# Ten weight places for the first two rounds, and the embedding products in the last group of experts

## The chip, the cores and the metric

The kernel runs on one core of a Trainium2 chip. Each core has five engines with instruction streams of their own: TensorE (PE, matrix products, with its weight loads shown as PEld), VectorE (DVE), ScalarE (ACT), GpSimd (POOL) and SyncE (SP). SP issues nearly all transfers here; sixteen DMA engines carry them out, in the order in which SP's queue hands them over. Engines meet through semaphores. Data on chip lie in SBUF (128 partitions), and matrix products are written to eight PSUM banks of 128 x 512 fp32.

The metric is the time of one execution in microseconds (us) on the device. It is given as a median of timed runs; a separate, profiled execution gives the trace.

## What is computed

256 tokens of width 1024, all in fp32, one layer:

```python
h = rms_norm(x, norm_mix_g)
proj = h @ w_in
x = x + concat([s5_mixer(proj[:, :512]), rwkv7_mixer(h, ...)]) @ w_out
# 32 experts, the best 4 for each token
hf = rms_norm(x, norm_moe_g)
logits = hf @ router_w + router_b
top_v, top_i = top_k(logits, 4);  gates = softmax(top_v)
for e in experts:                       # for the tokens that chose e
    gt  = minimum(xb @ w_gate[e] + b_gate[e], 7.0)
    up  = clip(xb @ w_up[e] + b_up[e], -7.0, 7.0)
    act = (up + 1.0) * gt * sigmoid(1.702 * gt)
    yb  = act @ w_down[e] + b_down[e]
    x  += gates[e] * yb
# the embedding of the layer, p is 256 x 256
gate = sigmoid(rms_norm(x, norm_ple_g) @ ple_w_gate)
x = x + (p @ ple_w_proj) * gate
out = rms_norm(x, final_norm_g)
```

An expert's three matrices are 1024 x 1024 fp32, 4 MB each. All 32 experts are read: 384 MB. (MB and KB are the profile's binary ones where a transfer's size is meant: 2048 KB is 2,097,152 bytes.)

## The kernel before

**Stages.** First the two mixers (a long program of small products), the output projection, the turned residual stream `x2T`, and the router's logits. Then `route_tensor`, `route_vector` and `route_scalar` choose the best four experts for each token and count the tokens. Then the experts run one after another. Then comes a tail: the third norm, the gate product with `ple_w_gate`, the last norm and the output.

**One expert** is `expert` in `expert_tensor` on PE: 16 contraction steps of gate products, 16 of up products, a `scatter` of the expert before into the banks 0 to 3 (they hold the sum over all experts until the tail), turns, a `gather` of the next expert's tokens, and 16 steps of down products. Each product with weights is written in two column halves of 64 tokens by 512. The first four experts are written out, groups 1 to 6 run in a loop on the register `q`, and the last four are written out again (group 7).

**Weights** come in chunks of 2 MB, half of a matrix: two of `w_gate`, two of `w_up`, two of `w_down` for each expert, so 192 chunks in all, numbered in the order of their use from 0. `arena` is one SBUF tile cut into 47 units of 4 KB per partition. `RING` names eight places of four units (`slot(0)` to `slot(7)`). A ninth place, `extra`, is made of the units 24, 25, 26 and 29 and is used once, for chunk 8: three quarters are issued in L358, the last in L1490 once the four embedding products are done, for unit 29 is a part of their weights. From chunk 9 on, `expert_sync` waits on SP until an earlier chunk is used (`chunks_used`, counted by PE) and issues the next one into its place: chunk i for i from 9 to 16 waits until i - 8 chunks are used, later ones until i - 7 are used.

**Before the experts** SP's order is: chunks 0, 4 and 5; the embedding's `pT` and `wproj`; the input again; chunk 1 after the recurrence (L348); chunks 6 and 7 after `mix_rw_ready` (L352); chunks 2 and 3 after the output projection (L355); the three quarters of chunk 8 after the logits (L358). The places of a later one overlap with data that the mixers still need.

**The embedding products** `ple_proj(n)` compute p @ ple_w_proj in four pieces of 128 x 512, two contraction steps each (the trace counts four fp32 instructions for one). Piece 2 stands on PE ahead of the second half of the logits, pieces 3 and 0 at the head of `route_tensor`, piece 1 in `open_outputs` behind the first expert's up products. ScalarE's `copy_ple` (L1343) moves each from its bank to SBUF, and `open_outputs` waits for all four copies, since it reuses the banks 0 to 3 for the down bias. Right behind it the first expert also runs a `scatter` of zeros.

**Small tiles.** The routing tables, `gT`, `pg`, `xg` and `y` of the experts lie in the units 37, 38 and 40.

## Time and profile before

| | |
|---|---|
| median of 3 timed runs | 1180.39 us (1180.38 to 1183.22) |
| profiled execution, its own time | 1182.24 us |
| its span in the trace | 1180.4 us |
| PE busy | 1104.3 us (94% of the span) |
| DVE, ACT busy | 359.5 us, 198.6 us |
| moved by DMA | 430.58 MB (decimal), mean 365 GB/s |
| mean granted TensorE clock | 0.998 of full speed |

The span is the trace from its first to its last instruction; the profiled execution's own time holds 1.84 us more that lies around it. A stretch of the span is named by its start and end in us. A row of the timeline gives start, duration, engine, line and operation; "idle before" is how long the engine stood still ahead of it, and what released it. SPq is SP's DMA issue: the duration there is that of issuing, not of the transfer. A row xN merges N instructions, and its duration then reaches from the first's start to the last's end. A window's row gives each engine's busy time with instruction counts, the granted clock of PE (1.00 is full speed), the busy share of the sixteen DMA engines and what they moved.

### The profile page before, as it was taken

The numbers are of one execution on the slowest core, as the hardware profiler recorded it, in microseconds if no ns is written. First come the engines' busy times: TensorE is split into PE (matmuls) and PEld (weight loads), VectorE is DVE, ScalarE is ACT, GpSimd is POOL, SyncE is SP. The second block draws the span as 40 slices with busy tenths as digits, with TensorE's granted clock in tenths as the row PEclk, the third lists the DMA queues.
The fourth block names the chain that finished last, engine by engine and source line by source line (L and its number), as shares of the span: only waits on it lengthen the run. The fifth ranks groups of instructions, "written<-read, shape, count | busy, mean of one in ns | idle before, by whom it ended". The sixth has DMA issues, their size and how long they took to land.

```text
span 1180.4 us, 16582 instructions
## 1 busy us (share of the span) xinstructions
PE 1104.3 (94%) x7042; PEld 480.1 (41%) x7042; DVE 359.5 (30%) x745; ACT 198.6 (17%) x318; POOL 5.8 (0%) x11
## 2 busy tenths in 40 slices
PE   9999999999999999999999999999999999999987
PEld 8788974433333333333333333333333333333334
DVE  7987745312222222212111222222111111111123
ACT  6761322310110000000000000000000000000022
POOL 0100000000000000000000000000000000000000
PEclk9999999999999999999999999999999999999999
DMA  9402284899999999999999999999999999999970
GB/s 325 134 2 78 88 328 154 362 393 401 428 428 428 428 427 429 429 428 428 429 429 429 428 428 429 429 428 428 429 429 428 428 428 431 428 426 428 428 300 36
DMA packets 44844, 430.58 MB, mean 365 GB/s; under 512 B 4992, under 2 KB 15616, under 8 KB 20096
## 3 DMA queue, kind: packets, MB, share of 16 engines
q1 hardware_dynamic: 44608, 429.40, 87.2%
q8 instruction: 36, 0.59, 0.2%
q0 software_dynamic: 192, 0.52, 0.1%
q14 instruction: 8, 0.07, 0.0%
HBM read 428.86 MB, written 1.05 MB: 364 GB/s over the span
## 4 chain that ended last, share of the span: by engine, by line
PE 50%; DMA 44%; DVE 4%; ACT 1%; issue 1%; SPq 0%; DVEq 0%; ACTq 0%
PE bank L1321 34%; DMA arena<-in_exp_w_up 24%; DMA arena<-in_exp_w_gate 19%; PE bank L249 13%; PE bank L1383 1%; DVE arena L638 1%; PE bank L1632 1%; PE bank L1628 1%; DMA arena<-in_xT 0%; ACT arena L475 0%; PE bank L984 0%; DVE arena L882 0%; DVE arena L629 0%; DVE arena L632 0%; PE bank L266 0%
## 5 line engine op out<-in xcount | busy, mean ns | idle before, releaser
L1321 PE MATMUL bank<-arena 128*64 128x512 f32 (+3 forms) x3808 | 849.7, 588 | 59.1 <-DMA arena<-in_exp_w_up 52.0
L1321 PEld LDWEIGHTS bank<-arena 128*64 128x64 f32 (+3 forms) x3808 | 272.4, 140 | 591.1 <-issue 471.6
L249 PE MATMUL bank<-arena 64*64 64x64 f32 (+8 forms) x2104 | 170.7, 265 | 7.1 <-issue 3.6
L249 PEld LDWEIGHTS bank<-arena 64*64 64x64 f32 (+3 forms) x2104 | 137.0, 146 | 35.9 <-issue 18.5
L1517 ACT ACTIVATE cc<-arena 128x512 f32<-128x512 f32 x32 | 20.2, 630 | 459.7 <-DVE arena L1562 459.7
L1567 DVE TENSOR_SCALAR arena<-bank 128x512 f32<-128x512 f32 x32 | 22.1, 692 | 219.9 <-PE bank L1321 219.9
L1364 DVE TENSOR_TENSOR arena<-bank,par 128x512 f32<-128x512 f32 x32 | 22.1, 692 | 216.7 <-PE bank L1383 216.7
L1562 DVE TENSOR_SCALAR arena<-bank 128x512 f32<-128x512 f32 x32 | 22.1, 692 | 163.4 <-PE bank L1321 163.4
L1522 ACT ACTIVATE arena<-bank 128x256 f32<-128x256 f32 x32 | 12.3, 383 | 313.9 <-PE bank L1628 313.9
L1577 DVE COPY arena<-bank 128x512 f32<-128x512 f32 x32 | 22.1, 692 | 98.7 <-PE bank L1321 98.7
L1377 ACT ACTIVATE rec<-bank 128x512 f32<-128x512 f32 x32 | 34.2, 1069 | 43.0 <-PE bank L1321 43.0
L1569 DVE SCALAR_TENSOR_TENSOR arena<-arena,cc 128x512 f32<-128x512 f32 x32 | 33.8, 1056 | 1.1
L1565 DVE TENSOR_TENSOR cc<-cc,arena 128x512 f32<-128x512 f32 x32 | 22.2, 692 | 24.5 <-ACT cc L1517 24.5
L1383 PEld LDWEIGHTS bank<-con,rec 128*128 128x128 f32 x128 | 13.4, 141 | 26.2 <-issue 25.1
L1383 PE MATMUL bank<-con,rec 128*128 128x128 f32 x128 | 21.0, 286 | 0.8 <-ACT rec L1377 0.8
L1524 ACT ACTIVATE arena<-bank 128x512 f32<-128x512 f32 x32 | 19.1, 597 | 1.7
L1549 DVE TENSOR_SCALAR arena<-con,arena 128x128 f32<-128x128 f32 x64 | 19.1, 341 | 0.9 <-issue 0.8
L1632 PE MATMUL bank<-con,arena 128*128 128x128 f32 x128 | 19.2, 273 | 0.0
L1360 DVE TENSOR_SCALAR arena<-con,arena,small 128x64 f32<-128x64 f32 x64 | 17.2, 311 | 6.7 <-DVE arena L1555 6.6
L1628 PEld LDWEIGHTS bank<-con,arena 128*128 128x128 f32 x64 | 6.4, 141 | 24.3 <-issue 24.3
L1632 PEld LDWEIGHTS bank<-con,arena 128*128 128x128 f32 x128 | 15.0, 140 | 0.0
L1628 PE MATMUL bank<-con,arena 128*128 128x128 f32 x64 | 14.0, 301 | 0.0
(278 smaller groups left out, 406.8 us busy)
## 6 DMA issues: line engine op xcount, KB each, us to landing
arena<-in_exp_w_gate SPq DMA_DIRECT2D x64, 2048.0 KB, 31.9
arena<-in_exp_w_down SPq DMA_DIRECT2D x63, 2048.0 KB, 35.4
arena<-in_exp_w_up SPq DMA_DIRECT2D x63, 2048.0 KB, 34.3
arena<-in_w_in SPq DMA_DIRECT2D x8, 1024.0 KB, 12.0
arena<-in_w_out SPq DMA_DIRECT2D x4, 1024.0 KB, 6.3
arena<-in_ple_w_gate SPq DMA_DIRECT2D x2, 2048.0 KB, 33.3
arena<-in_exp_w_down SPq DMA_DIRECT2D x2, 1024.0 KB, 34.5
arena<-in_exp_w_up SPq DMA_DIRECT2D x1, 1536.0 KB, 12.8
```

What stands on the lines that cost most here:

```text
L249: return nc.tensor.matmul(out, lhsT, rhs, start=start, stop=stop, skip_group_check=True)
L1321: return nc.tensor.matmul(out, lhsT, rhs, start=start, stop=stop, skip_group_check=True)
L1364: nc.vector.tensor_tensor(xg[:, :, :].rearrange("p (h k) s -> p k h s", h=2), GAT[:, :].rearrange("p (k h s) -> p k h s", h=2, k=4), prm(" ...
L1377: nc.scalar.activation(by_run(xc), plain(GAT[:, :]), ACT.Copy).then_inc(s["moved"], 1)
L1383: last = nc.tensor.transpose(GAT[:, k * P:(k + 1) * P], xc[:, k * P:(k + 1) * P], ident)
L1562: ts(gt, GATE[:, :], 7.0, None, ALU.min).then_inc(s["gt_ready"], 1)
L1565: tt(sg, sg, gt, ALU.mult).then_inc(s["swish_ready"], 1)
L1567: ts(up, UP[:, :], 7.0, -7.0, ALU.min, ALU.max).then_inc(s["swish_ready"], 1)
L1569: stt(by_run(gt), plain(up), 1.0, plain(sg), ALU.add, ALU.mult).then_inc(s["act_ready"], 1)
L1577: V.tensor_copy(y, YB[:, :]).then_inc(s["y_ready"], 1)
L1628: ins = nc.tensor.transpose(YB[:, t * P:(t + 1) * P], pg[:, t, :], ident)
L1632: ins = nc.tensor.transpose(GATE[:, k * P:(k + 1) * P], gt[:, k * P:(k + 1) * P], ident)
```

## The change

1. Chunk 8's place `extra[0]` is made of the units 24 to 27, and a tenth place `extra[1]` of the units 37, 38, 28 and 40 is added for chunk 9. Both are used a second time, for chunks 18 and 19. From chunk 20 on only the eight places of the ring are used. Chunk i for i from 10 to 27 waits on SP until i - 9 chunks are used, later ones until i - 7 are used.
2. Chunk 9 is issued before the experts in four pieces of 512 KB: two behind chunk 1, one behind chunks 6 and 7, one behind chunks 2 and 3. Chunk 8 is issued whole behind the logits.
3. The four embedding products leave the routing and the first expert. They stand in the first two experts of the last group (experts 28 and 29), one behind the gate products and one behind the up products of each, all into the bank `GAT`, each waiting for the copy of the one before. `wproj` and `pT` stay on chip until then.
4. The first expert's scatter of zeros is dropped, and two of VectorE's clearing writes with it.
5. The small tiles move out of the units 37, 38 and 40 into tiles of the mixers that are no longer needed (`s5p`, `power`, `coef`, `rec`) and into free parts of the units 41 and 42. `final_g` is read into unit 43 once one more chunk is used.

```diff
-        extra = [un(a) for a in (24, 25, 26, 29)]
+        extra = [[un(a) for a in places] for places in ((24, 25, 26, 27), (37, 38, 28, 40))]
...
                 sp.dma_start(slot(1), chunk_src(1, 0)).then_inc(chunk_in[1], 16)
+                for k, place in ((0, 37), (2, 28)):
+                    sp.dma_start(un(place), ahead[1][:, k * D:(k + 1) * D]).then_inc(extra_in[1], 16)
 
                 sp.wait_ge(s["mix_rw_ready"], 2)
                 for c in (6, 7):
-                    sp.dma_start(slot(c), chunk_src(c % NC, 1)).then_inc(chunk_in[c], 16)
+                    sp.dma_start(slot(c), chunk_src(c - 6, 1)).then_inc(chunk_in[c], 16)
+                sp.dma_start(un(40), ahead[1][:, 3 * D:4 * D]).then_inc(extra_in[1], 16)
                 sp.wait_ge(s["out_done"], 4)
                 for c in (2, 3):
                     sp.dma_start(slot(c), chunk_src(c, 0)).then_inc(chunk_in[c], 16)
+                sp.dma_start(un(38), ahead[1][:, D:2 * D]).then_inc(extra_in[1], 16)
                 sp.wait_ge(s["logits_done"], 1)
                 sp.wait_ge(s["x2_root"], 2)
-                sp.dma_start(un(24, 3), ahead[:, 0:3 * D]).then_inc(extra_in, 16)
+                sp.dma_start(un(24, 4), ahead[0]).then_inc(extra_in[0], 16)
...
-                pe.wait_ge(p_in, 48)
-                ple_proj(2, banks[2]).then_inc(s["ple_done"], 1)
...
     def route_tensor(pe):
-        pe.wait_ge(mixer["x2_ready"], 4)
-        ple_proj(3, banks[3]).then_inc(mixer["ple_done"], 1)
-        ple_proj(0, banks[0]).then_inc(mixer["ple_done"], 1)
...
     def open_outputs(pe):
 
-        ple_proj(1, banks[1]).then_inc(mixer["ple_done"], 1)
-        pe.wait_ge(s["ple_copied"], 4)
         for n in range(4):
...
+    FIRST = NSLOT + len(extra)
+
+    def ring_slot(i):
+
+        return (i - 2 * FIRST) % NSLOT
...
     def expert_sync(sp):
-        for i in range(NSLOT + 1, QUAD * NC):
-            sp.wait_ge(s["chunks_used"], i - NSLOT if i <= 2 * NSLOT else i - NSLOT + 1)
-            sp.dma_start(slot((i - 1) % NSLOT), chunk_src(i % NC, i // NC)).then_inc(chunk_in[(i - 1) % NSLOT], 16)
-            if i == NSLOT + 4:
-                sp.wait_ge(mixer["ple_done"], 4)
-                sp.dma_start(extra[3], ahead[:, 3 * D:4 * D]).then_inc(extra_in, 16)
+        for i in range(FIRST, 2 * FIRST + NSLOT):
+            sp.wait_ge(s["chunks_used"], i - FIRST + 1)
+            src = chunk_src(i % NC, i // NC)
+            if i == 2 * FIRST - 1:
+                sp.dma_start(un(37, 2), src[:, 0:2 * D]).then_inc(extra_in[1], 16)
+                for k, place in ((2, 28), (3, 40)):
+                    sp.dma_start(un(place), src[:, k * D:(k + 1) * D]).then_inc(extra_in[1], 16)
+            elif i == 2 * FIRST - 2:
+                sp.dma_start(un(24, 4), src).then_inc(extra_in[0], 16)
+            else:
+                c = i % FIRST if i < 2 * FIRST else ring_slot(i)
+                sp.dma_start(slot(c), src).then_inc(chunk_in[c], 16)
...
     def expert_scalar(act):
...
+            if embed is not None:
+                copy_ple(act, embed)
+                copy_ple(act, embed + 1)
...
                 ins.then_inc(s[done], 1)
+                if embed is not None:
+                    pe.wait_ge(p_in, 48)
+                    if embed + m:
+                        pe.wait_ge(s["ple_copied"], embed + m)
+                    ple_proj(embed + m, GAT).then_inc(mixer["ple_done"], 1)
 
             if q is None and place == 0:
-                open_outputs(pe)
-            pe.wait_ge(s["gT_ready"], n + 1)
-            pe.wait_ge(s["y_ready"], n + 1)
-            scatter().then_inc(s["scattered"], 1)
+                open_outputs(pe).then_inc(s["scattered"], 1)
+            else:
+                pe.wait_ge(s["gT_ready"], n + 1)
+                pe.wait_ge(s["y_ready"], n + 1)
+                scatter().then_inc(s["scattered"], 1)
```

On SP, from chunk 1 to the first transfers that wait for used chunks, before:

```order
L348 DMA arena<-in_exp_w_gate 128x4096
L352 DMA arena<-in_exp_w_gate 128x4096 x2
L355 DMA arena<-in_exp_w_up 128x4096 x2
L358 DMA arena<-in_exp_w_up 128x3072
L1487 DMA arena<-in_exp_w_up 128x4096
L1487 DMA arena<-in_exp_w_down 128x4096 x2
L1487 DMA arena<-in_exp_w_gate 128x4096
L1490 DMA arena<-in_exp_w_up 128x1024
```

and now:

```order
L350 DMA arena<-in_exp_w_gate 128x4096
L352 DMA arena<-in_exp_w_up 128x1024 x2
L356 DMA arena<-in_exp_w_gate 128x4096 x2
L357 DMA arena<-in_exp_w_up 128x1024
L360 DMA arena<-in_exp_w_up 128x4096 x2
L361 DMA arena<-in_exp_w_up 128x1024
L364 DMA arena<-in_exp_w_up 128x4096
L1499 DMA arena<-in_exp_w_down 128x4096 x2
```

Chunk 9, the second half of expert 1's `w_up`, was the first to wait (in L1487); now its four quarters stand among the transfers that wait for no used chunk, and the first that waits is chunk 10.

On PE, from the turns of `x2` to the first expert's turns, before (`lora_hidden` holds `pT`, so these rows are the embedding products; 128x32 are logits, `arena,con 128x32` the ranks, `rec` the gathered tokens):

```order
L266 MATMUL bank<-con,arena 128x128 x4
L249 MATMUL bank<-arena,lora_hidden 128x512 x2
L249 MATMUL bank<-arena 128x32 x8
L249 MATMUL bank<-arena,lora_hidden 128x512 x4
L1321 MATMUL bank<-arena,con 128x32 x5
L1321 MATMUL bank<-arena 64x512 x4
L1321 MATMUL bank<-con,arena 32x128 x4
L1383 MATMUL bank<-con,rec 128x128 x4
L1321 MATMUL bank<-arena 64x512 x36
L249 MATMUL bank<-arena,lora_hidden 128x512 x2
L1321 MATMUL bank<-arena 128x512 x8
L1628 MATMUL bank<-con,arena 128x128 x2
```

and now:

```order
L266 MATMUL bank<-con,arena 128x128 x4
L249 MATMUL bank<-arena 128x32 x8
L1326 MATMUL bank<-arena,con 128x32 x5
L1326 MATMUL bank<-arena,s5p 64x512 x4
L1326 MATMUL bank<-con,power 32x128 x4
L1382 MATMUL bank<-con,rec 128x128 x4
L1326 MATMUL bank<-arena 64x512 x16
L1326 MATMUL bank<-arena,s5p 64x512 x2
L1326 MATMUL bank<-arena 64x512 x16
L1326 MATMUL bank<-arena,s5p 64x512 x2
L1326 MATMUL bank<-arena,s5p 128x512 x4
L1650 MATMUL bank<-con,rec 128x128 x2
```

The embedding products are gone here, and the eight 128x512 products ahead of the first expert's turns (down bias and scatter) are four. They stand again on PE in the last group, in expert 28 and likewise in 29:

```order
L1326 MATMUL bank<-arena 64x512 x16
L1326 MATMUL bank<-arena,s5p 64x512 x2
L249 MATMUL bank<-arena,lora_hidden 128x512 x2
L1326 MATMUL bank<-arena 64x512 x16
L1326 MATMUL bank<-arena,s5p 64x512 x2
L249 MATMUL bank<-arena,lora_hidden 128x512 x2
L1326 MATMUL bank<-arena,coef 128x512 x4
```

In each of the two experts one embedding product now follows the gate products and one the up products, ahead of the scatter (`arena,coef`).

## Rows read from the trace of the kernel before

**Rows 1.** The page: GB/s in 40 slices, and the chain by engine.

```profile
GB/s 325 134 2 78 88 328 154 362 393 401 428 428 428 428 427 429 429 428 428 429 429 429 428 428 429 429 428 428 429 429 428 428 428 431 428 426 428 428 300 36
...
PE 50%; DMA 44%; DVE 4%; ACT 1%; issue 1%; SPq 0%; DVEq 0%; ACTq 0%
```

**Rows 2.** DMA issues: what, how many, KB each, median us from issue to landing.

```profile
arena<-in_exp_w_up SPq DMA_DIRECT2D x63, 2048.0 KB, 34.3
...
arena<-in_exp_w_up SPq DMA_DIRECT2D x1, 512.0 KB, 11.9
```

**Rows 3.** Windows: stretch, length, engines' busy us (instructions), clock, DMA share, GB/s.

```profile
224.00:300.00 76.00, 75.31 (x360) 26.35 (x358) 16.16 (x37) 8.63 (x13) 0.00 (x0) 1.00 0.93 379
...
300.00:1080.00 780.00, 730.92 (x3432) 246.49 (x3430) 158.13 (x352) 72.35 (x109) 0.00 (x0) 1.00 1.01 428
```

**Rows 4.** Windows of 4 us around the routing and the first experts.

```profile
192.00:196.00 4.00, 3.48 (x8) 1.63 (x9) 3.97 (x3) 0.00 (x0) 0.00 (x0) 1.00 0.00 0
...
224.00:228.00 4.00, 4.00 (x22) 1.36 (x20) 1.39 (x7) 0.00 (x0) 0.00 (x0) 1.00 0.07 28
...
248.00:252.00 4.00, 4.00 (x22) 1.45 (x20) 0.69 (x1) 0.00 (x0) 0.00 (x0) 1.00 0.84 258
...
276.00:280.00 4.00, 4.00 (x22) 1.55 (x24) 0.69 (x1) 0.00 (x0) 0.00 (x0) 1.00 0.89 307
```

**Rows 5.** Timeline of SP's issues: start us, us, line, what is loaded.

```profile
183.40 0.34 SPq L348 DMA_DIRECT2D arena<-in_exp_w_gate  x1
199.08 0.81 SPq L352 DMA_DIRECT2D arena<-in_exp_w_gate  x2
...
213.46 0.33 SPq L358 DMA_DIRECT2D arena<-in_exp_w_up  x1
227.15 0.33 SPq L1487 DMA_DIRECT2D arena<-in_exp_w_up  x1
...
239.78 0.33 SPq L1490 DMA_DIRECT2D arena<-in_exp_w_up  x1
249.64 0.33 SPq L1487 DMA_DIRECT2D arena<-in_exp_w_gate  x1
...
276.00 4.50 SPq L1487 DMA_DIRECT2D arena<-in_exp_w_gate  x2
...
328.92 4.44 SPq L1499 DMA_DIRECT2D arena<-in_exp_w_gate  x2
```

**Rows 6.** Line L1487's fifteen transfers of 2 MB.

```profile
DMA to landing us min/median/max: 8.0/10.8/16.0
```

**Rows 7.** Timeline of the routing.

```profile
212.65 0.16 DVE L930 RECIPROCAL small<-small 128x1 f32<-128x1 f32 x1 [4.02 <-ACT small L564]
...
213.27 3.68 PE L249 MATMUL bank<-arena,lora_hidden 128*128 128x512 f32 x8
...
213.57 0.41 DVE L1400 SCALAR_TENSOR_TENSOR arena<-bank,small,bb 128x32 f32<-128x32 f32 x2 [0.76 <-PE bank L249]
...
215.53 0.60 DVE L1414 TENSOR_REDUCE arena<-arena 128x64 f32<-128x256 f32 x1
...
216.78 1.20 PE L1321 MATMUL bank<-arena,con 128*128 128x32 f32 x10
```

**Rows 8.** Timeline of PE behind the first expert's up products.

```profile
237.77 1.98 PE L249 MATMUL bank<-arena,lora_hidden 128*128 128x512 f32 x4
...
240.44 3.06 PE L1321 MATMUL bank<-arena 32*128 32x512 f32 x16 [0.69 <-ACT arena L1343]
```

**Rows 9.** PE's waits from 520 to 1120: us in total, times, longest.

```profile
PE bank L1321 <- DMA arena<-in_exp_w_up: 46.3, 41, 1.2
```

**Rows 10.** Timeline of PE: the last expert's second up chunk.

```profile
1124.10 5.79 PE L1321 MATMUL bank<-arena 128*64 128x512 f32 x26 [1.24 <-DMA arena<-in_exp_w_up]
```

**Rows 11.** Windows of 1 us in the recurrence.

```profile
149.00:150.00 1.00, 0.22 (x6) 0.22 (x8) 0.00 (x0) 0.20 (x1) 0.00 (x0) 1.00 1.29 537
...
151.00:152.00 1.00, 1.00 (x3) 0.82 (x4) 0.00 (x0) 0.38 (x1) 0.00 (x0) 0.50 1.01 434
```

More of the change, by code:

```diff
@@ L291, in slot @@
             return un(RING[c], RUN)
[L293 to L294 removed]
+        ple = [un(26 + n // 2)[:, n % 2 * 512:(n % 2 + 1) * 512] for n in range(4)]
+        state_tables = [a.rearrange("p m n -> p (m n)") for a in (s5p,)] + [a.rearrange("p a b n -> p (a b n)") for a in (power, coef)]
+        ahead = [chunk_src((NSLOT + i) % NC, 1) for i in range(2)]
+        clear_expert_state, rest_sync, rest_scalar, rest_vector, rest_tensor = experts(nc, io, ctx, arena, con, par, banks, ring, slot, ahead, extra, sg, rec, ple, state_tables, chunk_in, extra_in, chunk_src, p_in, ple_proj, s, logits, inv, by_run, plain, x2, bias_parts, bias_down, rbias)
         with nc.Block() as block:
@@ L1307, in experts @@
-    nbase = un(38)[:, 425:426].bitcast(I32)
-    nlast = un(38)[:, 426:427].bitcast(I32)
+    gT = turned_gates.rearrange("p (t m) -> p t m", t=TT)
+    onehot = tables[:, 0:128].rearrange("p (t m) -> p t m", t=TT)
+    pick = tables[:, 128:160].bitcast(BF16)
+    gatesT = tables[:, 160:288]
+    st = tables[:, 288:320]
+    gates = counts[:, 0:64].rearrange("p (t e) -> p t e", t=TT)
+    rank = counts[:, 64:128].rearrange("p (t e) -> p t e", t=TT)
+    cnt, cflag = counts[:, 128:136], counts[:, 136:144]
@@ new lines, in experts @@
+    nbase = counts[:, 145:146].bitcast(I32)
+    nlast = counts[:, 146:147].bitcast(I32)
+    route = un(41)[:, 256:1024]
+    lg = route[:, 0:64].rearrange("p (t e) -> p t e", t=TT)
+    mask = route[:, 64:128].rearrange("p (t e) -> p t e", t=TT)
+    top = route[:, 128:144].rearrange("p (t e) -> p t e", t=TT)
+    topi = route[:, 144:160].bitcast(U32).rearrange("p (t e) -> p t e", t=TT)
+    topf = route[:, 160:176].rearrange("p (t e) -> p t e", t=TT)
+    ex = route[:, 176:192].rearrange("p (t e) -> p t e", t=TT)
@@ L1500, in expert_sync @@
-        for i in range(QUAD * NC - 1):
+                sp.dma_start(slot(ring_slot(i)), chunk_src(i % NC, e)).then_inc(chunk_in[ring_slot(i)], 16)
+        for i in range(begun, QUAD * NC - 1):
             sp.wait_ge(s["chunks_used"], base + (QUAD * NC + i - NSLOT + 1))
-            sp.dma_start(slot((i - 1) % NSLOT), chunk_src(i % NC, E - QUAD + i // NC)).then_inc(chunk_in[(i - 1) % NSLOT], 16)
-        end, last = (QUAD * NC - 2) % NSLOT, chunk_src(NC - 1, E - 1)
+            sp.dma_start(slot(ring_slot(i)), chunk_src(i % NC, E - QUAD + i // NC)).then_inc(chunk_in[ring_slot(i)], 16)
@@ L1528, in expert_scalar @@
         for place in range(QUAD):
-            expert(place, first=place == 0)
+            expert(place)
         act.wait_ge(s["counted"], 1)
@@ L1535, in expert_scalar @@
         for place in range(QUAD):
-            expert(QUAD * n_last + place, last=place == QUAD - 1)
+            expert(QUAD * n_last + place, place == QUAD - 1, 2 * place if place < 2 else None)
     def expert_vector(dve):
@@ L1660, in expert_tensor @@
         for place in range(QUAD):
-            expert(q, QUAD * q + place, NC * place, place == QUAD - 1)
+            expert(q, QUAD * q + place, NC * place, place == QUAD - 1, 2 * place if place < 2 else None)
         return n_last
```

108 lines of the change are left out of this document (47 added, 61 removed).

## The prediction, made before the changed kernel ran

> **What bounds the kernel now.** I read the page first. PE is busy for 94% of the span, and one could stop there. But the chain of work gives PE 50% and DMA 44%, and the GB/s row stands at 428 from slice 11 on, up to the tail [rows 1]. The windows confirm it: 428 GB/s over 780 us, with the sixteen engines' share at 1.01 [rows 3]. No rate stands above that for long, so 428 is this kernel's ceiling. At it a chunk (2.097 MB) takes 4.90 us and an expert 29.4 us.
>
> PE needs less. While the chunks are there it takes 26.5 us for an expert: the transfers issued at 276.00 and at 328.92 are released by the same step of PE two experts apart [rows 5]. So there are two regimes. Early on PE is the slower to start and eats a stock of chunks. Once that is eaten, it waits for DMA: 46.3 us in the 600 us from 520 to 1120, 2.3 us for each expert, always on an up chunk [rows 9]. The last such wait ends at 1124.10, at the last expert's second up chunk [rows 10]. Behind it lie 56.3 us that hang on nothing of DMA's.
>
> The end is therefore set by when the DMA stream gets through. The bytes are the same in both kernels. What counts is the **time in which DMA stands idle** before it is saturated, and every microsecond filled there comes off the end. An earlier PE by itself brings nothing. The reader is to see the idle stretches: 0 GB/s at 192 to 196, between chunk 1 (issued at 183.40) and chunks 6 and 7 (199.08); 28 GB/s at 224 to 228, when all that fits is loaded and the first chunk in use is freed only at 227.15; 258 GB/s at 248 to 252; 307 GB/s at 276 to 280 [rows 4, 5].
>
> **The sum, part by part.**
>
> *Pieces of chunk 9 ahead of 199.* Two of its four pieces (1.05 MB) now follow chunk 1 into a stretch with no traffic. At 428 GB/s that is 2.45 us of stream done in idle time. The other two pieces and chunk 8's last quarter (1.57 MB, 3.7 us) lengthen the busy queue that runs from 199 on. Its end moves from about 224.3 (the 0.07 share of the window from 224 on) to 228.0. The first expert's up chunks 2 and 3 are behind two of these pieces, 2.4 us later; they had been landed well before PE's need at some 230, so nobody waits.
>
> *Idle time from 224 to 300.* 76 us at 379 GB/s instead of 428 is 76 x (1 - 379/428) = 8.7 us lost before [rows 3]. With ten places the first chunk that waits is chunk 10, released when chunk 0 is used, at 227.15 before and earlier now. The queue then holds work until 228.0, so the gap closes, and from there chunk k starts at 228.0 + 4.90 (k - 10).
>
> *What comes back.* The stream is only unbroken if each chunk is issued in time. For that I need PE's new times. In the routing VectorE could read the second half of the logits once its scale is there, at 212.65 + 0.16; it started at 213.57, behind the embedding product that stood ahead of the logits: 0.76 us. The rank products then stood behind two more embedding products (end 216.95) though VectorE had their mask at 215.53 + 0.60: some 0.4 us more [rows 7]. In the first expert 240.44 - 237.77 = 2.67 us of product and copy go, and half of the 3.06 us behind it (the scatter of zeros), 1.5 us [rows 8]. Together 5.3 us; VectorE's two operations behind the up products are then just late by some 0.1, so **PE is 5.2 us earlier** from the first expert's turns on. Tight points: chunk 14 waits for five used chunks, which was so at 249.64, now 244.4, and starts at 247.6. Chunk 30, the third after the places fall back to eight, waits for 23 used chunks, which was so at 328.92, now 323.7, and starts at 326.0. The margins are 3.2 and 2.3 us. For what a margin does, the trace has one end: chunk 18 was issued at 276.00 with the queue just empty, and its window lost 4 x (1 - 307/428) = 1.1 us [rows 4, 5]. Two such points give 0 to 2.3 us; both margins are on the good side, so I take 0.7. Later the stock grows by 3 us for each expert.
>
> This gives 2.45 + 8.7 - 0.7 = 10.4 us. A second count goes by chunks: chunk 18 flowed from about 277.1 (issue and 1.1 us) and now from 228.0 + 8 x 4.90 = 267.2; 9.9 us, less the share of the 0.7 behind it, 9.2. I take the middle, **9.8 us**.
>
> *The embedding products in the last group.* Each takes 1.98 us [rows 8], two in expert 28 and two in 29: about 3.8 us each, 7.6 in all, on PE. PE has 2.3 us of waiting in each expert [rows 9]. It is late by 1.5 after 28, 3.0 after 29, 0.7 after 30, and in time in 31, whose last wait (1.24 us, [rows 10]) is behind all of them. Cost 0; without that cover it would be 7.6. The copies on ScalarE (0.6 us each) wait behind the sigmoid and are awaited by PE only at the next product or at the gather, with 7 us of up products or the scatter in between. A PE that is 3 us late also frees places 3 us late; transfers land 34.3 us after their issue [rows 2], seven deep, so the queue does not run dry.
>
> *The rest.* VectorE's two clearing writes stood while PE was still in the output projection: 0. The tiles moved within SBUF change no size of an operation: 0. final_g waits for one more chunk, and is needed 45 us later: 0.
>
> *Four pieces for one chunk.* The piece of 512 KB issued at 239.78 landed 11.9 us later, at 251.7 [rows 2, 5]. Four chunks flowing from 228.2 end at 247.8, and a chunk alone lands 8.0 us after its issue, 3.1 more than its 4.90 [rows 6]. So the piece flowed for at most 251.7 - 3.1 - 247.8 = 0.8 to 1.2 us, its bytes' share of 428 GB/s, and a split costs nothing in a filled queue. The Trainium skill ("SBUF — State Buffer", "The DMA setup-cost knee") speaks against splits: every transfer pays about 2 us that do not scale with its bytes. If that held up the queue, six more transfers would take back some 12 us and the change would lose; by the row it is latency, hidden where others are queued.
>
> **Rivals.**
>
> *A. The queue runs thin at chunks 14 and 30.* PE loses its lead if its clock falls. In the trace it did once: PE was busy for 0.22 us of 149 to 150, and at 151 the granted clock was 0.50, the 1.2 GHz level [rows 11]. The embedding products kept PE busy in the routing at full clock; without them it has nothing between the logits and the ranks, from some 212.6 to 215.6 by the times worked out above. If the clock falls there, the products up to the first expert's start double, and the lead shrinks from 5.2 to about 2.7 us; the margins are then 0.7 and -0.2 us, and some 2.3 to 3 us come back instead of 0.7: a gain of 7.5 to 8, so 1172.6. For it: the row. Against: the pause is barely as long as the thin stretch there, and two lost microseconds early reach the end only through the queue. The Trainium skill says so as a rule ("TensorE: Matmul & The Clock Gate", "What's actually happening"): the throttled state is the default and activity releases it.
>
> *B. The late products leak into the end.* If PE's waits were not all slack (the products around them are slowed too), up to 3 us stay: gain 6.8, 1173.6. For it: 7.6 of 9.2 us of slack are taken. Against: the last wait lies behind three experts that can catch up.
>
> *C. Slower: the stream itself.* Nine transfers instead of seven are queued for two rounds, and 181 chunks lie on the stream from chunk 10 on, 886 us. If its rate fell by 1.1%, below 423 GB/s, all is given back; at 420 the kernel takes 1187. Against: the rate was 428 whether few or seven transfers were queued.
>
> *D. It does not do what it says.* If the queue found no chunk to carry (the tenth place filled late), only the 2.45 us and a third of the idle time go: gain 2 to 3.5, 1177.6.
>
> **How the numbers follow.** The profiled execution took 1182.24 us, of which 1180.4 are its span; the sum makes 1172.4 of it, a span of 1170.6. The median of the timed runs, 1180.39, lies 1.85 below that execution, and the forecast is for such a median: 1180.39 - 9.8 = **1170.6**. Forecast as told, a gain of 8.6 to 11.2: 0.62. A: 0.20. B: 0.07. More than 11.2 (idle time elsewhere, or a quicker tail): 0.05. D: 0.04. C: 0.02. The range takes in the forecast, A and most of B and of the higher gains: 1168.6 to 1173.8. A measurement of this kernel tells about 0.3% (3.5 us) from no change: faster 0.94, same 0.04, slower 0.02.
>
> **What would show it.** In the new profile the windows from 224 to 300 should stand at 425 or more, 192 to 196 partly filled, the first rank product at about 215.6, chunk 10 issued at about 226, chunk 14 at 244 to 245, the last expert's second up chunk taken at about 1114.3, and 56.3 us behind it. A clock of 0.5 between 214 and 222 shows A; dips at about 247 and 326 give its price. Waits for DMA missing in expert 31 show B. A rate under 426 in the long stretch shows C. I am wrong in principle if the windows are full and the end does not move.

## The result, and the profile after

| | before | changed |
|---|---|---|
| median of the timed runs | 1183.22 us (7 runs, 1180.38 to 1183.49) | 1173.65 us (7 runs, 1169.81 to 1181.72) |
| ratio, 95% interval | | 0.9938, 0.9916 to 0.9959 |
| profiled execution, its span | 1182.24, 1180.4 us | 1173.44, 1171.6 us |
| mean granted clock of the profiled execution | 0.998 | 0.991 |

A second set on another chip gave 1176.40 us against 1181.24, a ratio of 0.9957 (0.9942 to 0.9973). The ratio is estimated from all fast runs and is not the quotient of the medians; one run of before in the second set, at 2922 us, is not among them. The changed kernel is faster, by 7.3 us in the first set and 5.1 in the second if the ratios are taken, by 9.6 and 4.8 if the medians are subtracted. The first set's medians flatter it: the seven runs of before lie in two groups, at 1180.4 and at 1182.1 to 1183.5, and their median falls in the upper one. The forecast was 9.8 us (ratio 0.9917), from a median of three runs of before that lay in the lower one. The changed kernel's runs also spread over 12 us where those of before spread over 3.

The page of the changed kernel: granted clock in tenths in 40 slices, GB/s in the same slices, and the chain by engine.

```profile
PEclk9899999899999999999999999999999999999999
...
GB/s 324 138 2 44 84 370 175 391 428 425 427 426 428 427 428 428 430 429 427 426 429 429 429 428 429 429 426 427 430 429 429 428 430 428 426 429 428 428 297 36
...
PE 52%; DMA 41%; DVE 4%; ACT 2%; issue 1%; SPq 0%; DVEq 0%; ACTq 0%
```

Against [rows 1] the stream reaches 428 two slices earlier (slice 9, not 11), as forecast. But two slices show a lowered clock, and the second of them (205 to 234 us) holds the routing; the first (29 to 59 us) lies in the mixers. The same stretch in windows (length, busy us of PE, PEld, DVE, ACT, POOL, clock, DMA share, GB/s):

```profile
192.00:196.00 4.00, 3.72 (x9) 1.81 (x10) 3.97 (x3) 0.00 (x0) 0.00 (x0) 1.00 0.14 55
...
208.00:212.00 4.00, 3.58 (x32) 3.44 (x31) 0.39 (x2) 2.18 (x6) 0.00 (x0) 1.00 1.02 428
212.00:216.00 4.00, 0.87 (x5) 0.79 (x4) 2.73 (x14) 2.25 (x6) 0.00 (x0) 0.63 0.99 416
216.00:220.00 4.00, 3.04 (x12) 1.95 (x13) 2.20 (x9) 0.00 (x0) 0.00 (x0) 0.50 1.01 434
...
224.00:228.00 4.00, 3.23 (x16) 1.20 (x18) 2.08 (x8) 0.69 (x1) 0.00 (x0) 1.00 0.90 376
228.00:232.00 4.00, 4.00 (x22) 1.36 (x20) 0.00 (x0) 0.00 (x0) 0.00 (x0) 1.00 0.74 221
...
244.00:248.00 4.00, 4.00 (x21) 1.34 (x19) 0.38 (x1) 0.68 (x1) 0.00 (x0) 1.00 0.98 418
248.00:252.00 4.00, 4.00 (x22) 1.42 (x20) 1.10 (x3) 0.00 (x0) 0.00 (x0) 1.00 1.04 438
...
224.00:300.00 76.00, 74.79 (x361) 26.14 (x362) 16.84 (x38) 8.74 (x13) 0.00 (x0) 1.00 0.99 414
300.00:1080.00 780.00, 740.46 (x3464) 250.78 (x3464) 159.77 (x360) 74.90 (x112) 0.00 (x0) 1.00 1.01 428
```

The dips of before at 248 and 276 [rows 4] are gone, and 224 to 300 runs at 414 GB/s, not 379 [rows 3]. One gap is left, around 228: 376 and 221 GB/s, which is 2.4 us of idle time and so nearly all that is left of it. From 213 to 223 PE ran at 1.2 GHz, the lower of its two levels. Its timeline there (start, duration, what, idle before):

```profile
211.00 1.08 PE L249 MATMUL bank<-arena 128*128 128x32 f32 x8 [0.42 <-ACT arena L576]
215.21 2.34 PE L1326 MATMUL bank<-arena,con 128*128 128x32 f32 x10 [3.13 <-DVE arena L1411]
218.51 3.68 PE L1326 MATMUL bank<-arena,s5p 128*64 128x512 f32 x8 [0.96 <-DVE s5p L1359]
...
224.77 7.09 PE L1326 MATMUL bank<-arena 128*64 128x512 f32 x32 [0.78 <-DVE arena L1363]
```

The ranks start at 215.21 (216.78 before [rows 7]), but take 2.34 us instead of 1.20; the gather takes 3.68 us instead of 1.94. So the first expert starts at 224.77, and not at 222. SP's issue of the first chunk that waits (chunk 10) follows:

```profile
183.15 0.34 SPq L350 DMA_DIRECT2D arena<-in_exp_w_gate  x1
...
228.47 3.76 SPq L1499 DMA_DIRECT2D arena<-in_exp_w_down  x2
```

It comes at 228.47, even later than before (227.15, [rows 5]), when the queue is already empty. At the other end PE waits for DMA in the last expert as before [rows 10]:

```profile
1110.42 3.65 PE L1326 MATMUL bank<-arena 128*64 128x512 f32 x16 [1.02 <-DMA arena<-in_exp_w_up]
...
1115.31 3.65 PE L1326 MATMUL bank<-arena 128*64 128x512 f32 x16 [1.24 <-DMA arena<-in_exp_w_up]
```

Behind 1115.31 lie 56.3 us, as behind 1124.10 before. So DMA still sets the end, the products in the last group cost nothing, and the difference is made in the stream before 300.

### The profile page after: what moved, and what is told of

It reads as the page before. It is cut to its first block, busy times and chain, and to the rows that moved or that the text cites. A ratio compares the mean times of both kernels' runs of the same rounds, so it can differ in the third digit from the quotient of the medians.

```text
span 1171.6 us, 16573 instructions
## 1 busy us (share of the span) xinstructions
PE 1105.4 (94%) x7034; PEld 483.0 (41%) x7034; DVE 358.6 (31%) x745; ACT 199.5 (17%) x318; POOL 5.4 (0%) x11
## 4 chain that ended last, share of the span: by engine, by line
PE 52%; DMA 41%; DVE 4%; ACT 2%; issue 1%; SPq 0%; DVEq 0%; ACTq 0%
PE bank L1326 37%; DMA arena<-in_exp_w_up 24%; DMA arena<-in_exp_w_gate 17%; PE bank L249 12%; PE bank L1382 1%; DVE arena L644 1%; PE bank L1654 1%; PE bank L1650 1%; PE bank L990 0%; DMA arena<-in_xT 0%; ACT arena L481 0%; DVE arena L888 0%; DVE arena L635 0%; DVE arena L638 0%; PE bank L266 0%
## 5 line engine op out<-in xcount | busy, mean ns | idle before, releaser
L1326 PE MATMUL bank<-arena 128*64 128x512 f32 (+1 forms) x3152 | 714.7, 593 | 45.2 <-DMA arena<-in_exp_w_up 41.2
L1326 PEld LDWEIGHTS bank<-arena 128*64 128x64 f32 (+1 forms) x3152 | 227.0, 138 | 495.3 <-issue 400.3
L1326 PE MATMUL bank<-arena,s5p 128*64 128x512 f32 (+2 forms) x392 | 89.5, 541 | 1.0 <-DVE s5p L1359 1.0
L1579 DVE TENSOR_SCALAR rec<-bank 128x512 f32<-128x512 f32 x32 | 22.1, 692 | 211.4 <-PE bank L1326 211.4
L1574 DVE TENSOR_SCALAR arena<-bank 128x512 f32<-128x512 f32 x32 | 22.1, 692 | 162.3 <-PE bank L1326 162.3
L1326 PE MATMUL bank<-arena,coef 64*128 64x512 f32 x256 | 63.6, 615 | 0.8 <-DVE arena L1589 0.8
L1326 PEld LDWEIGHTS bank<-arena,s5p 128*64 128x64 f32 (+2 forms) x392 | 23.6, 130 | 44.1 <-issue 43.1
L1326 PEld LDWEIGHTS bank<-arena,coef 64*128 64x128 f32 x256 | 22.0, 186 | 36.4 <-issue 34.7
L1581 DVE SCALAR_TENSOR_TENSOR arena<-rec,cc 128x512 f32<-128x512 f32 x32 | 33.8, 1056 | 1.1
L1561 DVE TENSOR_SCALAR rec<-con,power 128x128 f32<-128x128 f32 x64 | 19.1, 342 | 0.7 <-issue 0.7
```

What stands on the lines that cost most here:

```text
L1326: return nc.tensor.matmul(out, lhsT, rhs, start=start, stop=stop, skip_group_check=True)
L1574: ts(gt, GATE[:, :], 7.0, None, ALU.min).then_inc(s["gt_ready"], 1)
L1579: ts(up, UP[:, :], 7.0, -7.0, ALU.min, ALU.max).then_inc(s["swish_ready"], 1)
L1581: stt(by_run(gt), plain(up), 1.0, plain(sg), ALU.add, ALU.mult).then_inc(s["act_ready"], 1)
```

## The experiments

**The account used for all of them.** If DMA sets the end, then a kernel's span is the time at which chunk 1 is issued (all ahead of it is the mixers' and varies between executions), plus the time the stream stands idle from 224 to 300 (76 us times 1 - GB/s / 428), plus a constant. The constant should be the same for all kernels with the early pieces, 2.45 us more without them. The rows for ten places in one round and for the doubled products each rest on a single run of their kernel.

| kernel, profiled execution | span | chunk 1 issued | GB/s 224 to 300 | idle us | constant | clock in the routing |
|---|---|---|---|---|---|---|
| before | 1180.4 | 183.40 | 379 | 8.7 | 988.3 | full |
| changed | 1171.6 | 183.15 | 414 | 2.5 | 986.0 | fell |
| changed, second set | 1175.1 | 183.65 | 396 | 5.7 | 985.8 | fell |
| three products put back | 1168.8 | 182.15 | 422 | 1.1 | 985.6 | full |
| the same, second set | 1172.2 | 185.32 | 422 | 1.1 | 985.8 | full |
| mixers filled too | 1170.8 | 183.72 | 422 | 1.1 | 986.0 | full |
| two put back | 1173.9 | 182.69 | 397 | 5.5 | 985.7 | fell |
| one, ahead of the logits | 1178.2 | 185.86 | 389 | 6.9 | 985.4 | fell |
| two, behind the logits | 1173.9 | 184.55 | 411 | 3.0 | 986.3 | fell |
| unread products in all pauses | 1177.0 | 184.00 | 386 | 7.5 | 985.5 | fell |
| early pieces issued late | 1174.5 | 186.19 | 425 | 0.5 | 987.8 | full |
| ten places, one round | 1180.5 | 184.88 | 370 | 10.3 | 985.3 | fell |
| last group's products doubled | 1174.6 | 182.13 | 401 | 4.8 | 987.7 | fell |
| nine places | 1174.6 | 179.66 | 390 (220 to 296) | 6.7 | 988.2 | fell |

Ten traces give 985.3 to 986.3, while their spans differ by 12 us. The four that stand out are those that should: before, the late pieces and the nine places, which have no early pieces, by 2.3, 2.0 and 2.2 us over the changed kernel's 986.0 or 985.8 (2.45 expected), and the doubled products. The nine places' window is set 4 us earlier, as its chunk 1 is.

Chunk 1's issue itself differs by 6.5 us between these traces. The clock also falls in the mixers, at about 52, at about 152, at both or at neither: with neither, chunk 1 was issued at 179.66 (nine places), with one of them at 182.13 to 184.55, with both at 184.88 to 186.19. (The kernel with its mixers filled, told below, has neither, but has more work there.) So a kernel's time holds two things, the mixers' part and the routing's, and the mean clock of a run does not tell them apart.

**Is it the clock? Three products put back.**

```diff
                 turn_x2(1, 1).then_inc(s["x2_turned"], 1)
+                pe.wait_ge(p_in, 48)
+                ple_proj(2, banks[2])
                 for k in range(KD):
...
     def route_tensor(pe):
+        ple_proj(3, banks[3])
+        ple_proj(0, banks[0])
```

> The changed kernel, with three embedding products issued once more at their old places on PE (one ahead of the second half of the logits, two at the head of the routing). Their results are overwritten; the real ones still stand in the last group. Theory T (the pause of PE between logits and ranks lets its clock fall, the first expert starts late, chunk 10 is issued late and DMA runs dry): granted clock 1.00 from 212 to 224, first expert starts at about 223.4 instead of 224.8, chunk 10 issued at about 227.1 instead of 228.5, idle DMA time from 226 to 230 halves, time 1 to 1.5 us below the changed kernel's, and a spread of the runs near that of the kernel before (3 us, against 12). Rival U (the late start comes from the longer waits of the routing itself, not from the clock): these products put back 1.2 us of routing, the first expert starts at 226, time 1 us above the changed kernel's.

Measured: 1171.3 us (1168.43 to 1173.08), ratio 0.9908 (0.9893 to 0.9922), granted clock 0.997 or 0.998 in each of five runs. PE's timeline, a window and SP's issue of chunk 10:

```profile
208.60 1.88 PE L249 MATMUL bank<-arena,lora_hidden 128*128 128x512 f32 x4
...
215.54 1.20 PE L1328 MATMUL bank<-arena,con 128*128 128x32 f32 x10
...
222.20 7.09 PE L1328 MATMUL bank<-arena 128*64 128x512 f32 x32 [0.78 <-DVE arena L1365]
```

```profile
216.00:220.00 4.00, 3.03 (x23) 1.26 (x22) 2.88 (x13) 0.33 (x1) 0.00 (x0) 1.00 1.05 442
...
224.00:300.00 76.00, 75.57 (x368) 26.45 (x366) 15.89 (x33) 8.04 (x12) 0.00 (x0) 1.00 1.00 422
```

```profile
225.90 3.76 SPq L1503 DMA_DIRECT2D arena<-in_exp_w_down  x2
```

PE does 5.6 us more work in the routing and yet starts the first expert 1.6 us earlier after chunk 1's issue (40.05 us against 41.62). The ranks take 1.20 us again. Theory T holds and rival U falls. Even with the clock held, 1.1 us stay idle at the same place: chunk 10 is issued at 225.90, and its bytes flow some 1.1 us later, when this trace's queue, loaded about 1 us earlier, has run dry. To be sure that no difference of chips is read, both kernels ran once more on one chip:

> The changed kernel itself, on the chip of the three others of this set, so that they can be held against it. Its granted clock is expected at 0.986 to 0.995 with runs spread over 6 us or more, 1172 to 1176 in the median, 6 to 9 us below the kernel before.

> The kernel with three embedding products issued once more at their old places, again, beside the changed kernel on one chip. Theory T (the clock's fall in the routing is what is missing of the forecast): clock 0.996 or more in every run, spread 4 us or less, 2 to 4 us below the changed kernel's median. Rival V (the difference seen so far lies between chips or in the mixers): within 1 us of it.

Measured: 1176.40 us (clock 0.986 to 0.992) and 1173.32 us (clock 0.996 or 0.997). The difference of 3.1 us is as expected, though with four runs against seven the intervals of the two ratios just overlap (0.9906 to 0.9948, 0.9942 to 0.9973); the spread of the latter (1170.06 to 1175.13) was larger than the 4 us named, so not all of the spread comes from the routing. The trace of the changed kernel in this set shows how far the fall can reach:

```profile
224.00:228.00 4.00, 3.21 (x10) 1.32 (x12) 2.08 (x8) 1.19 (x1) 0.00 (x0) 0.50 0.99 421
228.00:232.00 4.00, 4.00 (x14) 1.15 (x12) 0.00 (x0) 0.00 (x0) 0.00 (x0) 0.59 0.07 25
```

Here PE still runs at 1.2 GHz while the first expert's products start (225.74), chunk 10 is issued at 232.15, and DMA is idle for 5.7 us instead of 2.5. In the seven runs of the first set the time falls and rises with the clock: 1169.81 us at 0.994, 1172.44 at 0.993, 1173.44 and 1173.65 at 0.991, 1176.25 and 1176.36 at 0.990, 1181.72 at 0.986. The pair of traces shows that the clock's return, which comes sooner or later in the first expert, is a part of the spread. How large a part is not shown: only one run of each set has a trace, and the longer ones may have lost time in the mixers as well.

**Which pause is it?** Four kernels fill less, or elsewhere. In the first, `fill(n)` issues n unread products of 128x512:

```diff
     def route_tensor(pe):
+        fill(7)
...
+        fill(2)
         pe.wait_ge(s["hot_ready"], 2)
         gather()
...
+        fill(1)
         turn_gathered(pe, 0)
+        fill(2)
```

> The changed kernel, with matrix products that nobody reads in every pause of PE in the routing: 7 of 128x512 between logits and ranks, 2 ahead of the gather, 1 and 2 around the turns of the gathered tokens. Theory T: clock 1.00 from 212 to 224, first expert starts at about 222.3, chunk 10 issued at 226, no idle DMA time from 226 to 230 (420 GB/s or more), time 2.5 us below the changed kernel's median, about 1171, spread of the runs 3 us. Rival U: no gain, chunk 10 at 228 or later. Rival V (the spread and the missing microseconds come from clock falls in the mixers, ahead of 200): clock there falls in some runs as before, the gain is under 1 us and the spread stays at 10 us or so.

Measured: 1175.66 us, ratio 0.9943: no better than the changed kernel. But these seven products were more than the pause could hold. At full clock six instructions of this form take 2.74 us, as in the kernel before:

```profile
203.80 2.74 PE L249 MATMUL bank<-arena 128*128 128x512 f32 x6
```

The seven are 14 instructions, some 6.2 us against a pause of 3.1, so they would have held the ranks up at full clock too. This run shows when the clock falls, and not what a fitting cover of the pause is worth. The others put back one product ahead of the logits, two behind them, or one and one. Against the kernel with three put back, each of the three pieces below is what one of them takes out, in this order:

```diff
-        ple_proj(3, banks[3])
-        ple_proj(0, banks[0])
...
-                ple_proj(2, banks[2])
...
-        ple_proj(0, banks[0])
```

> The changed kernel, with one embedding product issued once more at its old place ahead of the second half of the logits (its result is overwritten), and nothing between logits and ranks. Theory T1 (the thin stretch begins with the logits' products of 32 columns, and it is the wide product among them that held the clock): clock 1.00 from 208 to 224, ranks at about 215.0, chunk 10 issued some 0.5 us earlier than with three products (225.4 by that trace's clock), time as with three products, 1171, or 0.5 less. T2 (the pause between logits and ranks alone is what lets the clock fall): it falls as in the changed kernel, chunk 10 at 228 or later, time 1173 to 1176.

> The changed kernel, with two embedding products issued once more at the head of the routing, between logits and ranks, and none ahead of the logits. T1: the clock falls at about 212, the two products then take up to 7 us instead of 3.7 and hold the ranks up until 217 to 219, chunk 10 is issued at 229 or later, time 1174 or more. T2: the pause is filled, the clock stays at 1.00, time about 1171.

> As with three products at their old places, but only one of them stands between logits and ranks (1.98 us in a pause of 2.2 us) and one ahead of the logits. If the clock holds, ranks start 0.5 us earlier and the idle time at 224 shrinks: equal to the three products or 0.5 us faster. If the shorter cover lets the clock fall, as with one product ahead alone: runs up to 1177 and a clock of 0.993 or less.

Measured: 1175.66 us (ratio 0.9943, 0.9924 to 0.9961), 1174.72 (0.9933, 0.9913 to 0.9953) and 1172.6 (0.9923, 0.9908 to 0.9939). In all three traces the clock falls. PE's timelines, of the unread products, of the two behind the logits, and of one ahead:

```profile
213.57 8.72 PE L1326 MATMUL bank<-arena 128*128 128x512 f32 x14
```

```profile
213.82 6.54 PE L249 MATMUL bank<-arena,lora_hidden 128*128 128x512 f32 x8
```

```profile
214.02 1.87 PE L249 MATMUL bank<-arena 128*128 128x32 f32 x16
218.63 2.34 PE L1328 MATMUL bank<-arena,con 128*128 128x32 f32 x10 [2.73 <-DVE arena L1413]
```

Seven products that take some 6.2 us at full clock took 8.7, and two that take 3.68 took 6.5: with nothing wide ahead of the logits the clock had fallen at 211.9 and 212.8, ahead of the filler, which then began at half speed and held the ranks up, to 222.12 and 220.19. (Two further traces with the changed kernel's own order of PE agree that the fall can come before the pause or in it: 210.4 with the doubled products, 213.0 in the changed kernel's.) With one product ahead and none behind, it fell at 217.6, 1.7 us into the pause, and came back only in the first expert, at about 234.6, so that DMA stood still from 231 to 236:

```profile
228.00:232.00 4.00, 3.35 (x8) 1.01 (x10) 1.98 (x8) 0.10 (x1) 0.00 (x0) 0.50 0.61 258
232.00:236.00 4.00, 4.00 (x16) 1.18 (x14) 0.00 (x0) 0.00 (x0) 0.00 (x0) 0.67 0.00 0
```

So neither T1 nor T2 alone: both stretches have to be covered, the logits' products and the pause behind them. The case with one product on each side is not settled. Its trace is that of its slowest run (1175.72 us) and shows a fall at 216.9; the other three runs have clocks of 0.995 and 0.996 and 1171.45 to 1173.3 us, and its median is as good as with three products on the same chip (1173.32). A cover that begins after the fall does not bring the time back: 0.9943 and 0.9933 are no better than the changed kernel's 0.9938, nor are they clearly worse.

**What the early pieces are worth.** On the kernel with three products put back:

```diff
-                for k, place in ((0, 37), (2, 28)):
-                    sp.dma_start(un(place), ahead[1][:, k * D:(k + 1) * D]).then_inc(extra_in[1], 16)
...
                 sp.dma_start(un(24, 4), ahead[0]).then_inc(extra_in[0], 16)
+                for k, place in ((0, 37), (2, 28)):
+                    sp.dma_start(un(place), ahead[1][:, k * D:(k + 1) * D]).then_inc(extra_in[1], 16)
```

> As the kernel with three products at their old places, but the two pieces of chunk 9 that stood behind chunk 1 are issued behind chunk 8. Theory: 2.45 us of the stream leave idle time ahead of 199 and lengthen the queue that runs dry at about 226; there they fill the 1.35 us that were idle between 220 and 232, so 1.1 us are lost: about 1172.4 against 1171.3. Rival (pieces in an idle stretch cost more than their bytes, or help the first expert): equal or faster, or over 2.5 us slower.

Measured: 1174.31 us, 3.0 and 1.0 above that kernel's two medians (1171.3, 1173.32), all on different chips, and behind mixers that were 4 us later in the profiled execution than in the first of them. By the times the rival of over 2.5 us is not ruled out. The trace is the better judge: span less chunk 1's issue is 988.3 against 986.65 and 986.9, so 1.4 to 1.65 us lost, and the gap at 228 nearly closed:

```profile
224.00:300.00 76.00, 74.00 (x361) 26.13 (x360) 16.95 (x40) 10.19 (x15) 0.00 (x0) 1.00 1.01 425
```

2.45 us leave the early idle stretch and 0.6 come back at 228. The expected 1.1 was a little low; the mechanism holds: bytes moved into idle time are worth their time at 428 GB/s, once.

**What the second round is worth.** Ten places, used once; from chunk 10 on the ring:

```diff
-        for i in range(FIRST, 2 * FIRST + NSLOT):
-            sp.wait_ge(s["chunks_used"], i - FIRST + 1)
+        for i in range(FIRST, QUAD * NC):
+            sp.wait_ge(s["chunks_used"], i - FIRST + 1 if i < FIRST + NSLOT else i - NSLOT + 1)
+            sp.dma_start(slot(ring_slot(i)), chunk_src(i % NC, i // NC)).then_inc(chunk_in[ring_slot(i)], 16)
```

> The changed kernel, with ten places for the first round only; from chunk 10 on the eight places of the ring are used. Theory (a filled queue is worth what the released chunks allow): chunk 18 then waits for 11 used chunks, 273.4 in the changed kernel's trace, while the stream would want it at 268.7 to 269, so DMA stands idle for 4 to 6 us at about 270 to 275, and less at 277 to 290; the span is 5 to 7 us longer than the changed kernel's. Rival (the second round buys nothing, since PE's speed sets the releases anyway): within 1.5 us of it.

Measured, in one run: 1182.3 us, a span of 1180.5, no faster than the kernel before (1181.83 in this set). The windows show the new gap where chunk 18 waits (it is issued at 276.80):

```profile
272.00:276.00 4.00, 4.00 (x22) 1.30 (x20) 0.00 (x0) 1.16 (x2) 0.00 (x0) 1.00 0.22 90
276.00:280.00 4.00, 4.00 (x22) 1.43 (x20) 0.69 (x1) 0.00 (x0) 0.00 (x0) 1.00 0.59 160
```

5.7 us are lost in these 8 us, 6.3 with the two windows behind, and span less chunk 1's issue is 7.2 us above the changed kernel's. Some 1.7 us more than in the changed kernel are lost between 224 and 236, where the clock fell a second time. So the second round is worth some 6 us, most of what the change gives.

**What moving the products is worth without the tenth place.**

```diff
-    FIRST = NSLOT + len(extra)
+    FIRST = NSLOT + 1
```

(with the early pieces of chunk 9 left out and the ring taking over at chunk 9)

> The changed kernel without its tenth place: chunk 8's place is used once, chunk 9 is the first that waits for a used chunk, the ring of eight takes over from there; embedding products in the last group, small tiles moved, as in the changed kernel. Theory: the queue ends at about 224.7, chunk 9 flows from 229.6 (clock fallen in the routing), so 5 us idle; the later gaps shrink since PE is 2.6 us earlier than in the kernel before; 224 to 300 loses 6.5 us against 8.7, so 2 to 3.5 us faster than the kernel before, 1178 to 1180. Rival (moving the products is worth nothing, the places are all of it): within 1 us of the kernel before. Second rival (the clock's fall costs more than the move gives): slower than it.

Measured: 1183.04 us (10 runs, 1176.4 to 1185.32), ratio 1.0005 (0.9988 to 1.0022): nothing. The profiled run was its fastest (a span of 1174.6, chunk 1 issued as early as 179.66), and there the gap ahead of chunk 9 shows:

```profile
220.00:224.00 4.00, 3.22 (x18) 1.26 (x19) 2.08 (x8) 1.19 (x1) 0.00 (x0) 1.00 0.41 172
224.00:228.00 4.00, 4.00 (x22) 1.32 (x20) 0.00 (x0) 0.00 (x0) 0.00 (x0) 1.00 0.54 135
```

By the account this trace is 2.1 us better than before (span less chunk 1's issue 994.9 against 997.0), as I expected. The timed runs are not, and seven of the ten have a clock of 0.987 to 0.990. So the first rival is right in the time. The likely reason is the second one's, that longer falls of the clock take the gain back, but no trace of one of the longer runs shows it. The profiled run owes its short span to the mixers: its clock held there throughout.

**How much room the last group has.** Each of the four products there issued twice:

```diff
+                    ple_proj(embed + m, GAT)
                     ple_proj(embed + m, GAT).then_inc(mixer["ple_done"], 1)
```

> The changed kernel, with each of the four embedding products in the last group issued twice (15.2 us of PE instead of 7.6; the result is the same). If PE's waits for DMA there are all slack (2.3 us for each expert), PE is 5.3 late after expert 28, 10.6 after 29, 8.3 after 30, 6 in 31: the last expert's second up product ends 5 to 6 us later against the DMA stream and the span grows by 5 to 6 us, with no DMA wait left in expert 31. Rival B (the products already leak): 7.6 us or more.

Measured, in one run: 1176.39 us, a span of 1174.6, of which the account puts down 1.9 us to PE (987.7 against 985.8), not 5 to 6. No wait for DMA is left in the last expert, whose four gate and up chunks run through, as does the one before it; PE's timeline:

```profile
1088.54 7.04 PE L1326 MATMUL bank<-arena 128*64 128x512 f32 x32
...
1114.90 7.04 PE L1326 MATMUL bank<-arena 128*64 128x512 f32 x32
1121.77 0.39 PE L1326 MATMUL bank<-arena,s5p 128*64 128x512 bf16 x2
```

The eight products take four times 3.63 us from start to start of what follows (1021.10 to 1024.73), so 14.5 us and not 15.2, and the four experts had some 14.5 - 1.9 = 12.6 us of room, 3.2 each. The waits that the trace shows (2.3 us for each expert, [rows 9]) are not all of it: an expert takes PE some 26.4 us when nothing is missing (1088.54 to 1114.90 here) and 29.4 when DMA sets the pace, and that difference of 3.0 is nearly the room. Rival B had no ground.

**Would filling the mixers bring more?** On the kernel with three products put back:

```diff
                 lora_second_g()
+                for _ in range(3):
+                    mm(banks[4][:, :], lora2[:, 0:P], lora2[:, 0:512], True, True)
...
+                for _ in range(3):
+                    mm(banks[4][:, :], ident, con[:, 0:512], True, True)
                 pe.wait_ge(s["xy_ready"], 2 * LEVELS)
```

> As with three products at their old places, with three more unread products of 128x512 in each of two pauses of PE in the mixers: ahead of the eight norm sums at 50 us, and ahead of the recurrence at 147 us. Theory: the clock then holds at 52 to 60 and at 150 to 158 too (it fell at one or both in every trace so far), chunk 1 is issued at 181 to 182.5 instead of 182 to 186, and 1 to 2.5 us come off against the kernel with three products; clock 0.999. Rival: these products lengthen the path at full clock by as much as they save, within 0.7 us.

Measured: 1172.67 us (1171.34 to 1173.27), clock 0.997 to 0.999. In the trace the clock holds all the way to the tail, and the spread is down to 2 us. But chunk 1 is not issued earlier:

```profile
183.72 0.34 SPq L350 DMA_DIRECT2D arena<-in_exp_w_gate  x1
```

The rival is right for the median: what the clock gives back, the filler takes. (The expectation's remark that every trace before had a fall in the mixers is not so: the nine places' trace had none, and its chunk 1 at 179.66 shows what a clock held without filler is worth.) The kernel with three products put back (0.9908 and 0.9927 against before), this one (0.9926) and the one with a product on each side (0.9923) are the fastest of this study; in the same set they lie 3.1 to 3.8 us below the changed kernel's median.

## Why the prediction was right or wrong, point by point

- **What bounds the kernel: right.** DMA's stream at 428 GB/s sets the end in thirteen of the fourteen traces, all but the one with doubled products, with 56.3 us behind the last up chunk.
- **The early pieces, 2.45 us: right.** The window at 192 now carries 55 GB/s, and the late pieces cost 2.0 us by the account's constant.
- **The idle time from 224 to 300, 8.7 us before: right as a size.** 6.2 of them are gone in the profiled execution, 3.0 in that of the second set, 7.6 with the clock held.
- **What comes back, 0.7 us: wrong.** This is the step that failed. The stream was idle for 2.5 and 5.7 us where the sum had 0.7, so 1.8 and 5.0 us of the gain are missing. I looked for the thin places at chunk 14 and chunk 30 and gave them margins of 3.2 and 2.3 us. Nothing is lost there: 418 and 438 GB/s around 248, and 428 from 300 on. Chunk 10 was passed over: by my own numbers it would be issued at about 226 for a queue that ends at 228.0, less 1.1 us until it flows, so its margin was 0.9 us and the smallest of the three. And the lead on which all three rest was not there. PE was to be 1.2 us earlier at the first expert and was 1.3 us later in the profiled execution, since its clock had fallen in the routing. With the clock held by three products put back, 1.1 us are idle instead of 2.5 or 5.7, and that kernel and the one with the mixers filled too gain 8.6 to 10.9 us against before by their ratios, around the 9.8 that I forecast for a full clock.
- **The time: inside the range by luck.** 1173.65 us lies 0.15 below the range's upper end, which was set there for rival A; 1176.40 us of the second set lies outside. And the difference of the first set's medians, 9.6 us, comes near to 9.8 only because the median of before fell among its longer runs.
- **Rival A was the right mechanism at the wrong place, and in the second set too cheap.** It had the fall of the clock in the routing and a chance of 0.20, and charged it at chunks 14 and 30 with 2.3 to 3 us back. In all nine traces in which the products' old places are not all filled with products, the clock fell; in the four of the changed order in which they are, and in the kernel before, it held in the routing. The price came at chunk 10: 2.5 us of idle time in the first set, which is A's size, and 5.7 in the second, where the half clock lasted into the first expert. The argument against it, that the pause is barely as long as the thin stretch in [rows 11], counted idle time alone. The logits' products ahead of the pause belonged to the stretch, as the fillers behind them show: they began when the clock had already fallen.
- **The Trainium skill on the clock** ("TensorE: Matmul & The Clock Gate", "What's actually happening"): the default is throttled and activity releases it. By that rule the products in the routing were not only work but what kept the clock. The traces agree: ranks of 1.20 us with them, 2.34 without. I weighed it as a rival, and with that rule at hand it should have had more than 0.20.
- **The Trainium skill on small transfers** ("SBUF — State Buffer", "The DMA setup-cost knee"): the Trainium skill puts about 2 us on every transfer, whatever its size. The change adds four transfers of weights (nine for chunks 8, 9, 18 and 19, where there were five), not the six of the prediction. By the figure of the Trainium skill four cost 8 us, an estimate, if none of it is hidden. The traces do not agree with that: the rate is 428 GB/s as before, and the constant fell by 2.3 us where 2.45 were expected, so at most some tenths of a us are left for them.
- **The products in the last group, 0 us: right**, with more room than I gave them (12.6 us, not 9.2).
- **C and D: not seen.** The stream's rate is 428 from 300 to 1080 in every trace.
- **The reference.** The forecast of 1170.6 stood on a median of three, 1180.39; with seven and more runs before is 1181.2 to 1183.2. A gain is better judged by the ratios of all runs: 9.8 us forecast, 7.3 and 5.1 measured.

## What to carry to other kernels

Where a stream of transfers sets the end, add up its idle time and nothing else: each part of a change is worth what it fills, and the margin to check first is that of the first transfer that waits for a released place. Before you move matrix products out of a stretch in which TensorE has little to do, ask what they did for its clock; if the clock was full with them, put the price of the whole stretch at half speed, to its far end, into the sum. A stand-in must begin before the thin stretch does and must fit into the pause; one that began after the fall ran at half speed and held up the work behind it.

## What the runs showed of the hardware

- The granted clock fell at or soon after the logits' products (128x32), which have one pause of 0.42 us among them: at 211.9 with the unread products, when PE had been busy for 3.58 of the 4 us from 208 to 212, and in the changed kernel, with the same 3.58, at 213.0, 0.9 us into the next pause. The busy share of that window gave no warning.
- It returned after 7 to 17 us (212.8 to 219.6 with two products behind the logits, 217.6 to 234.6 with one ahead). At 1.2 GHz the gather takes 3.68 us, at 2.4 GHz 1.94.
- Ten traces of different kernels keep span less the first issue less the stream's idle time within 1.0 us. In a kernel that DMA bounds, one subtraction of this kind tells more than medians that differ by less than their spread.
